# A hybrid encoder layer on one core: reordered head slots in the mixers, and the adaLN modulation in two parts

## What is computed

```python
mod = jax.nn.silu(c) @ w_ada + b_ada                 # (2 requests, 6 * 1024)
sh1, sc1, g1, sh2, sc2, g2 = jnp.split(mod[:, None, :], 6, axis=-1)
h = _rmsnorm(x, norm1_w) * (1.0 + sc1) + sh1
proj = h @ w_in                                      # cq, ckv, kr, z, xbc, dt
y_attn = _mla(...)        # 8 heads, 128-query blocks over all keys, softmax, rms norm
y_ssd = _ssd_mixer(...)   # conv, two chunked scans (forward, backward), gate, rms norm
x = x + g1 * (jnp.concatenate([y_attn, y_ssd], axis=-1) @ w_out)
...
return x + g2 * _ec_moe(h, w_router, w_gate, w_up, w_down)
```

## Time and profile before

| | us |
|---|---|
| median of three runs | 3434.69 (3433.72 to 3434.99) |
| the profiled execution | 3435.31 |
| its span, first to last instruction | 3432.0 |
| TensorE busy in the span | 3030.9 (88%) |
| VectorE busy | 2099.8 (61%) |
| ScalarE busy | 1479.3 (43%) |
| mean granted TensorE clock | 0.936 of full |

### The profile page before, as it was taken

The page is one execution under the profiler, slowest core; times in us unless marked ns, Lnnn a source line. Parts: engine busy times, 40 slices in busy tenths (PEclk is TensorE's granted clock), DMA queues, the critical chain, the costliest instruction groups (busy, mean ns, idle before and its releaser), DMA issues. The chain is left out here.

```text
span 3432.0 us, 50059 instructions
## 1 busy us (share of the span) xinstructions
PE 3030.9 (88%) x17384; PEld 2426.6 (71%) x17384; DVE 2099.8 (61%) x3894; ACT 1479.3 (43%) x2832; POOL 176.7 (5%) x180
## 2 busy tenths in 40 slices
PE   8899933877898869937999999999999999999993
PEld 1577721553565645517999999999999999999993
DVE  0111085554555533377777887788778877887784
ACT  0111042344444332205555555555555555555552
POOL 0000000100000100000000000000000000000001
PEclk9899967898999889968999999999999999999997
DMA  9100023000001023307777776777677777777774
GB/s 348 71 25 12 0 91 108 13 32 34 31 20 38 20 93 117 128 25 260 231 232 245 250 231 221 252 238 239 223 244 241 240 225 238 244 239 233 227 228 156
DMA packets 353625, 544.46 MB, mean 159 GB/s; under 512 B 11264, under 2 KB 282880, under 8 KB 353536
## 3 DMA queue, kind: packets, MB, share of 16 engines
q1 hardware_dynamic: 344640, 511.83, 44.7%
q0 software_dynamic: 8896, 31.46, 3.9%
HBM read 492.13 MB, written 51.12 MB: 158 GB/s over the span
## 5 line engine op out<-in xcount | busy, mean ns | idle before, releaser
L2016 PE MATMUL banks<-rowsT_parts,weights_high 128*128 128x384 f32 x4096 | 1189.0, 362 | 12.3 <-DVE hidden_parts L1947 7.3
L2017 PE MATMUL banks<-rowsT_parts,weights_low 128*128 128x192 f32 x4096 | 1027.3, 251 | 0.0
L2016 PEld LDWEIGHTS banks<-rowsT_parts,weights_high 128*128 128x128 f32 x4096 | 770.0, 188 | 21.5 <-DVE hidden_parts L1947 9.9
L2017 PEld LDWEIGHTS banks<-rowsT_parts,weights_low 128*128 128x128 f32 x4096 | 783.3, 191 | 1.4
L2027 PE MATMUL banks<-weights_high,hidden_parts 128*128 128x512 f32 x1536 | 436.3, 392 | 0.0
L1934 DVE TENSOR_TENSOR gate_up_sums<-banks,gate_up_sums 128x192 f32<-128x192 f32 x512 | 181.6, 355 | 333.2 <-ACT gate_up_sums L1852 333.2
L1852 ACT ACTIVATE gate_up_sums<-banks 128x192 f32<-128x192 f32 x512 | 165.2, 323 | 463.4 <-PE banks L2017 457.8
L2027 PEld LDWEIGHTS banks<-weights_high,hidden_parts 128*128 128x128 f32 x1536 | 283.4, 188 | 70.1
L2027 PE MATMUL banks<-weights_low,hidden_parts 128*128 128x512 f32 (+1 forms) x1024 | 319.3, 393 | 0.0
L1884 DVE TENSOR_TENSOR weights_low<-slab_up,weights_high 128x1024 fp32r<-128x1024 f32 x256 | 311.9, 1219 | 0.0
L1884 DVE TENSOR_TENSOR weights_low<-slab_down,weights_high 128x1024 fp32r<-128x1024 f32 x256 | 311.6, 1217 | 0.0
(11 more groups left out here) (254 smaller groups left out, 3587.1 us busy)
## 6 DMA issues: line engine op xcount, KB each, us to landing
slab_gate<-w_gate SPq DMA_DIRECT2D x128, 1024.0 KB, 5.5
slab_up<-w_up SPq DMA_DIRECT2D x128, 1024.0 KB, 7.4
slab_down<-w_down SPq DMA_DIRECT2D x128, 1024.0 KB, 4.9
arena_modulation<-w_ada SPq DMA_DIRECT2D x12, 2048.0 KB, 9.3
arena_modulation<-ssd_tiles SPq DMA_DIRECT2D x12, 960.0 KB, 5.3
arena_modulation<-x_sample SPq DMA_DIRECT2D x16, 512.0 KB, 3.9
arena_modulation<-w_in SPq DMA_DIRECT2D x2, 3424.0 KB, 19.7
mixed<-arena_modulation SPq DMA_DIRECT2D x12, 512.0 KB, 2.9
```

The lines of the kernel that those rows point to most:

```text
L2016: nc.tensor.matmul(out[:, 0:2 * CT], w_hi[:, u, block], x[:, k, :], start=k == 0, stop=False)
L2017: mm = nc.tensor.matmul(out[:, 0:CT], w_lo[:, u, block], x[:, k, 0:CT], start=False, stop=k == KD - 1)
```

## The change

**Modulation.** The first block loads four slabs (columns 0 to 2047: shift 1 and scale 1) and then w_in. For a slab the products become 8 x 4 (`mod_rows`): 128 moving columns each, the four quarters of the slab going to partitions 0, 32, 64 and 96 of a bank. A 128 x 128 copy and one transpose then give the columns (`mod_columns`). The other eight slabs (gate 1, and the three of the second norm) are loaded, multiplied and turned beside the projections of tiles 2 to 9, through one buffer, banks 6 and 7.

**Mixers.** `seg` 0 and 1 stand in slot 0, 2 and 3 in slot 1; `off` 0 in slot 2, `off` 1 and `diag` in slot 3; `gate` in slot 5; `y_stats` in 5, `norm_y` in 6, `turn_y` and `mix_y` in 7, all in their own tile. `front` steps 1 to 6 stand in slots 0 to 5, and Q_STATS moves to slot 7 of the tile two ahead. `back_o` writes into `b_oT`, and `turn_o` moves from slot 7 to slot 6. The sizes of these pieces stay as they are.

```diff
+def mod_rows(nc, bank, silu, slab, k0, k1):
+    for k in range(k0, k1):
+        for q in range(4):
+            mm = nc.tensor.matmul(bank[32 * q:32 * q + 2, 0:P], silu[:, k, :], slab[:, k, P * q:P * q + P],
+                                  start=(k == 0), stop=(k == KD - 1))
+    return mm
```

In the projections, the sync queue's program:

```diff
                 load_tile(sp, x[j], x_of, g, r, x_in[j])
+                n = late(g)
+                if n is not None:
+                    if not (isinstance(n, int) and n == 0):
+                        sp.wait_ge(late_mm, n)
+                    sp.dma_start(slab, w_ada[:, :, bass.ds(n * 512 + 2048, 512)]).then_inc(slab_in, 16)
```

DVE's `back`:

```diff
+                n = late(g)
+                if n is not None:
+                    dve.wait_ge(late_mm, n + 1)
+                    nc.vector.tensor_copy(rows, core.ps[6][:, 0:P]).then_inc(late_out, 1)
                 dve.wait_ge(xbc_done, g + 1)
```

TensorE's `back`:

```diff
                 mm.then_inc(z_done, 1)
+                n = late(g)
+                if n is not None:
+                    pe.wait_ge(slab_in, n * 16 + 16)
+                    if not (isinstance(n, int) and n == 0):
+                        pe.wait_ge(late_done, n)
+                    mod_rows(nc, core.ps[6], core.silu_c, slab, 0, KD).then_inc(late_mm, 1)
                 pe.wait_ge(banks_dve, g + 1)
...
+                if n is not None:
+                    pe.wait_ge(late_out, n + 1)
+                    nc.tensor.transpose(core.ps[7][:, 0:P], rows, core.ident).then_inc(late_turned, 1)
```

In the mixers, TensorE's body of a tile:

```diff
                     turn_p(g, h, 0)
-                    if h < 4:
-                        seg(g, h, g - 1 if before or r else None)
-                    elif h == 4:
-                        off(g, j, more)
-                    elif h == 5:
-                        diag(g)
-                    elif h == 7:
-                        turn_y(g)
-                    if more and h < 7:
-                        front(h, g + 1, i + 1, 1 - j, g - 1 if before else None)
+                    if h < 2:
+                        seg(g, 2 * h, g - 1 if before or r else None)
+                    if h == 3:
+                        off(g, j, 1, more)
+                    if more and h < 6:
+                        front(h + 1, g + 1, i + 1, 1 - j)
                     turn_p(g, h, 1)
...
+                    if h < 2:
+                        seg(g, 2 * h + 1, None)
+                    if h == 2:
+                        off(g, j, 0, more)
+                    if h == 3:
+                        diag(g)
+                    if before and h == 6:
+                        turn_o(g - 1, 1 - j, more)
+                    if h == 7:
+                        turn_y(g)
```

More of the change, by code:

```diff
@@ L256, in modulation @@
     slab_in = [sem(f"ada_slab_in{s}") for s in range(SLABS)]
[L257 to L261, removed]
+    silu_c, consts_in, cleared = sem("silu_c"), sem("consts_in"), sem("mod_cleared")
+    rows_mm, rows_out, turned = sem("mod_rows_mm"), sem("mod_rows_out"), sem("mod_turned")
+    rows = [A.at(A_MODT + P * b, P) for b in range(2)]
     w = io["w_ada"][0].rearrange("(k p) n -> p k n", p=P)
@@ L290, in _ @@
             pe.wait_ge(silu_c, 1)
[L291 to L305, removed]
+            pe.wait_ge(cleared, 1)
+            for s in range(SLABS):
+                pe.wait_ge(slab_in[s], 16)
+                if s > 1:
+                    pe.wait_ge(rows_out, s - 1)
+                mod_rows(nc, core.ps[s % 2], core.silu_c, ring[s], 0, KD).then_inc(rows_mm, 1)
+                if s:
+                    pe.wait_ge(rows_out, s)
+                    nc.tensor.transpose(core.ps[2 + (s - 1) % 2][:, 0:P], rows[(s - 1) % 2], core.ident).then_inc(turned, 1)
@@ L307, in _ @@
+            pe.wait_ge(rows_out, SLABS)
+            nc.tensor.transpose(core.ps[2 + (SLABS - 1) % 2][:, 0:P], rows[(SLABS - 1) % 2], core.ident).then_inc(turned, 1)
         @block.vector
         def _(dve):
-            order = Order(dve, dve_order)
-            dve.sem_inc(rows_done, SLABS)
+            order = Order(dve, sem("mod_dve_order"))
             nc.vector.memset(core.eps[:, 0:1], EPS)
             nc.vector.memset(core.eps[:, 1:2], 1.0)
[L313 to L317, removed]
@@ L318, in _ @@
[L318 to L329 removed]
+            for b in (0, 1):
+                nc.vector.memset(core.ps[b][:, 0:P], 0.0)
@@ new lines, in _ @@
+            nc.vector.memset(core.ps[6][:, 0:P], 0.0).then_inc(cleared, 1)
+            dve.wait_ge(consts_in, 64)
+            for s in range(SLABS):
+                dve.wait_ge(rows_mm, s + 1)
+                if s > 1:
+                    dve.wait_ge(turned, s - 1)
+                nc.vector.tensor_copy(rows[s % 2], core.ps[s % 2][:, 0:P]).then_inc(rows_out, 1)
+                if s:
+                    dve.wait_ge(turned, s)
+                    mod_columns(nc, core, core.ps[2 + (s - 1) % 2], s - 1)
@@ L356, in projections, with late @@
     b_nat, b_z, b_x = core.ps[2], core.ps[3], core.ps[4:6]
+    slab, slab_in, rows = A.at(A_SLAB, KD, 512), sem("late_slab_in"), A.at(A_MODT, P)
+    late_mm, late_out, late_turned, late_done = (sem(n) for n in ("late_rows_mm", "late_rows_out", "late_turned", "late_cols"))
+    w_ada = io["w_ada"][0].rearrange("(k p) n -> p k n", p=P)
+    def late(g):
+        return g - 2 if not isinstance(g, int) or 2 <= g < 10 else None
     with nc.Block() as block:
```

160 lines of the change are left out of this document (92 added, 68 removed).

## The result

| | us |
|---|---|
| before, median | 3434.84 (3433.72 to 3438.39, 4 runs) |
| changed kernel, median | 3353.13 (3348.79 to 3361.72, 4 runs) |
| ratio | 0.976, 95% interval 0.974 to 0.979 |
| forecast | 3385, range 3346 to 3415 |

The change takes 82 us off, 2.4%; 50 were forecast. The profiled execution of the changed kernel is the slowest of its four, 3361.72 us with a span of 3360.1, so the two traces differ by 72 us only.

The account below looks back on a forecast made before the run. TensorE's program was taken to set the time in modulation, projections and mixers. From 3435.3 us, -14 for modulation with projections (-58 + 28 + 2.4 + 0.8 + 13) and -36 for both mixers gave 3385, range 3346 to 3415.

Parts of the forecast that it names:

- The head start: Modulation: with four slabs ahead instead of twelve, the first token tile is in at 47.5 us instead of 105.87, -58 us.
- The late slabs: Projections, tiles 2 to 9: eight slabs at 3.5 us each add 28 us, switches 2.4 and transposes 0.8.
- The new wait in the projections: Tiles 4 to 10 load behind a 2 MB slab, so TensorE waits 1.9 us seven times, 13 us.
- The waits of a sample tile: Sample mixer, tiles 2 to 7: TensorE waits 4.75 us a tile in place of 5.95, a gain of 1.2.
- The clock of a sample tile: Sample tiles 2 to 7: the clock, mean 0.91, costs 4.9 us a tile; 2.45 stays, near 0.95.
- I give back half: Sample mixer: half of the 4.9 us a tile lost to the clock stays lost, 2.45 us.
- The prompt mixer: Prompt mixer: 114.8 us work, 24.6 waits and 9 lost clock make 148.4 instead of 160.40, -12 us.
- Both unknowns fall well: Rival, chance 0.20: slab quarters overlap at 1.7 us a slab and both mixers' clock stays up, 3347 us.
- my own case: The forecast's main case, chance 0.52: 3385 us, with a range for it alone of 3368 to 3402.
- nothing to measure: Rival, chance 0.05: late slabs as dear as 3413 us, mixers only trade waits without the clock, about 3432.
- Slower: Rival, chance 0.07: waits in mixer slots 5 to 7 send TensorE to the lower clock for longer, 3446 us.

## Why the forecast was right, and where it was off

- **The head start.** -58 us were forecast, 58.5 measured: the transfers ahead of the first token tile were the right term, and tile 0 came in at 47.34 us against 47.5.
- **The late slabs.** A term that was mis-sized. I took the pace of the P.V products, 0.054 us a pass; four offsets gave 0.026. A steady tile with a slab takes 29.72 us, 25.83 + 1.42 of wait + 2.47, where I had 3.9. Eight make 19 us instead of 31. "TensorEngine Tiling (Array Packing)" of the Trainium skill, "Key Properties", says that tiles work independently, for which the forecast had 1.7 us a slab; the trace agrees with 1.64. The 0.76 us idle ahead of the slab's weight loads is the same as ahead of the P.V products; the price of the switch by itself no run measured, the 2.47 us hold products, switch and transpose.
- **The new wait in the projections.** 13 us in seven forecast, 12.1 in seven measured, and the run with the token tile first showed the cause. My terms as written give 12.5 - 10.88 = 1.6 us a wait, 11 in seven; the 1.9 and 13 of the forecast do not follow from them. The projections ended 27 us earlier, 14 forecast; the difference is nearly all the slabs.
- **The waits of a sample tile.** 4.75 us forecast, 3.3 measured. 0.45 at `diag` (0.65), 1.0 for the P.V products (1.2), 1.9 for ACT's copies (2.8 and 0.1). Each was in its place.
- **The clock of a sample tile.** "I give back half" was the second mis-sized term: all of it came back, 1.00 against my 0.95. That is 2.45 us a tile, 15 in six. I had counted three waits close together in slots 6 and 7 as a danger. They are 0.5 to 1.0 us each and the clock stayed; the run with the longer wait at `diag` shows that 1 us more ahead of the diagonal products is enough to bring half of the falls back.
- **The prompt mixer.** -12 us forecast, -2 in the traces. The waits were right (21.5 us against 24.6 by the same list), the clock was not: 0.85 costs 23.6 us of 157, where I had 9. This was the third mis-sized term. In the ten profiles of kernels with the new slots it lies between 0.85 and 0.97. Waits of 2.3 us ahead of the P.V products are the longest that come in every tile, and of the two mixers this is the one whose clock falls; but the same code of the mixer gave 0.86 and 0.92, so the cause of the single value stays open.
- **The rivals and the range.** "Both unknowns fall well", 3347, is close to what happened: the quarters overlapped and the sample clock stayed up, only the prompt clock didn't. The measured 3353 lies outside the 3368 to 3402 that I gave for my own case; the wider range holds it because it was drawn over that rival, and the miss at the prompt clock, 10 us the other way, kept the total from going further. The sum of "nothing to measure" was wrong: its terms, 3413 + 36 for the mixers - 7, give 3442 and not 3432. "Slower" did not happen, but the experiment at `diag` showed its mechanism at work, 17 us and more for one moved instruction.
- **What I left out.** I counted nothing for stretches that the change does not touch. The stages ahead of the prompt mixer took back 5.8 us, which the run with the mixers alone shows too. The experts gave 5.3: from TensorE's first to its last product there they take 1801.6 and 1802.3 us in the two profiles with the old modulation and 1796.1 to 1798.6 in the ten with the new. No run shows the cause of either, and they happen to cancel.
- **What stays open.** The traces differ by 72 us and the medians by 82; the profiled execution of the changed kernel, 3361.72, is itself 8.6 us above its median. The prompt mixer took 143 to 159 us over the ten profiles with the new slots; I can't say what made the other executions shorter.

## What to carry to other kernels

Read a wait not only by its length: 1 us more ahead of a run of small products on TensorE cost another 3.2 us through the clock in three of six tiles. When a wait is taken away, follow the three or four instructions behind it on each engine, since the next one waits in the same place; here the gate, then `y_stats`, then the exponentials. And when a large transfer is slipped in beside a loop, issue the loop's own load ahead of it, not behind the event that frees its buffer.

## What the runs showed of the hardware

- Products with two output columns at four partition offsets in turn ran side by side: by TensorE's product rows 1.93 us for 64 passes, 0.030 us a pass, against 7.15 us, 0.112 a pass, with one offset. By the weight loads it is 0.026 us a pass, against 0.054 with 64 columns at two offsets.
- With a TensorE wait of 0.41 to 0.51 us ahead of the diagonal products the granted clock was 1.00 in sample tiles 2 to 7 of nine profiles with the new slots. With 1.38 to 1.47 us, the only edit, it fell in three of these six tiles. In the kernel before, with 1.55 to 1.65 us, the diagonal products ran partly at the lower level in each of the six (4.68 to 6.50 us instead of 3.76), and with the modulation alone in five of them.
- The wait at this place is not the whole of it. In the prompt mixer it is 0.66 us in all four tiles of these nine profiles, and the diagonal products of the second tile still ran partly at the lower level (4.6 to 4.7 us) in five of them.
